# Reordering of raw weight buffers, of the next tokens' splits and of the output tokens' last scaling at a block's seam

## The reference

```python
mod = silu(c) @ ada_w + ada_b                       # shift, scale, gate
h = rms_norm(x, norm_w) * (1.0 + scale) + shift
p = h @ w_in                                        # 1024 x 5136: gq gk gv gz glr hq hf hi hz mg
# two chunk-wise gated linear states (chunks of 64), each normed, scaled and gated: o_g, o_h
g_a, g_b = split(sigmoid(mg + merge_b))
m = g_a * (o_g @ w_up_gla) + g_b * (o_h @ w_up_hgrn)
x = x + gate * (m @ w_out)
return rms_norm(x, final_norm_w)                    # y * rsqrt(mean(y*y) + eps) * final_norm_w
```

## Time and profile before

| | us |
|---|---|
| median of 3 runs | 2870.38 |
| lowest, highest | 2867.75, 2871.15 |
| the profiled execution | 2872.56 |
| its span | 2870.8 |
| TensorE busy in it | 2812.6 (98%) |
| VectorE, ScalarE, GpSimd busy | 1649.1, 1353.0, 312.5 |
| transfers | 373.11 MB, mean 130 GB/s |
| mean granted TensorE clock | 0.992 of full speed |

### The profile page before, as it was taken

One profiled execution on the slowest core, in us unless ns is written; L12 is line 12 of the kernel. 1 busy time (PEld: TensorE's weight loads), 2 busy tenths in 40 slices (PEclk: granted clock), 3 DMA queues, 4 the chain that ended last, 5 costly groups with the idle time before them and its releaser, 6 DMA issues.

```text
span 2870.8 us, 38281 instructions
## 1 busy us (share of the span) xinstructions
PE 2812.6 (98%) x14328; PEld 2302.4 (80%) x14328; DVE 1649.1 (57%) x2122; ACT 1353.0 (47%) x1763; POOL 312.5 (11%) x415
## 2 busy tenths in 40 slices
PE   7999999999999999999999999999999999999998
PEld 4878878788887888878888888788887888888886
DVE  7765475644656455564565636646366463755636
ACT  4643347434573345633456434564345643455423
POOL 1531100101001010010100110001100011000101
PEclk9999999999999999999999999999999999999999
DMA  8532362234522345223543235422354223532234
GB/s 333 206 129 96 125 214 91 79 103 136 204 89 82 105 157 181 91 79 103 180 160 96 74 107 190 148 94 74 124 177 142 95 74 125 191 133 89 74 99 150
DMA packets 100673, 373.11 MB, mean 130 GB/s; under 512 B 11440, under 2 KB 11696, under 8 KB 98928
## 3 DMA queue, kind: packets, MB, share of 16 engines
q1 hardware_dynamic: 97040, 358.62, 37.3%
q0 software_dynamic: 3168, 11.54, 1.1%
q10 hardware_dynamic: 256, 0.20, 0.0%
HBM read 345.99 MB, written 24.12 MB: 129 GB/s over the span
## 4 chain that ended last, share of the span: by engine, by line
issue 68%; PE 23%; POOL 6%; DVE 1%; DMA 1%; ACT 0%; POOLq 0%; SPq 0%; DVEq 0%; ACTq 0%
PE F L1223 8%; PE A L1212 8%; PE A L1274 3%; POOL rstd L460 2%; PE A L1296 1%; POOL rstd L457 1%; DMA ada_w<-in_ada 1%; POOL y_rs L460 1%; PE F L1212 1%; POOL m_raw L527 0%; POOL x_rs L460 0%; POOL m_raw L529 0%; POOL m_raw L525 0%; POOL m_raw L531 0%; DVE w_lo L822 0%
## 5 line engine op out<-in xcount | busy, mean ns | idle before, releaser
L822 DVE TENSOR_TENSOR w_lo<-w_raw,w_hi 128x1024 fp32r<-128x1024 f32 x528 | 653.4, 1240 | 930.4 <-ACT w_hi L576 927.2
L576 ACT ACTIVATE w_hi<-w_raw 128x1024 fp32r<-128x1024 f32 x528 | 556.3, 1057 | 669.2 <-PE A L1212 350.1
L1223 PE MATMUL F<-h_hi,w_hi 128*128 128x512 f32 x1408 | 553.8, 393 | 0.0
L1223 PE MATMUL F<-h_lo,w_hi 128*128 128x512 f32 x1408 | 548.2, 389 | 0.0
L1223 PE MATMUL F<-h_hi,w_lo 128*128 128x512 f32 x1408 | 548.2, 389 | 0.0
L1212 PE MATMUL A<-w_hi,h_hi 128*128 128x512 f32 (+1 forms) x1408 | 533.3, 379 | 0.0
L1212 PE MATMUL A<-w_lo,h_hi 128*128 128x512 f32 (+1 forms) x1408 | 523.7, 372 | 0.0
L1212 PE MATMUL A<-w_hi,h_lo 128*128 128x512 f32 (+1 forms) x1408 | 522.9, 371 | 0.0
L1212 PEld LDWEIGHTS A<-w_hi,h_hi 128*128 128x128 f32 x1408 | 264.9, 188 | 55.8 <-issue 8.7
L1223 PEld LDWEIGHTS F<-h_hi,w_hi 128*128 128x128 f32 x1408 | 264.4, 188 | 56.1 <-ACT gates L690 1.4
L1223 PEld LDWEIGHTS F<-h_lo,w_hi 128*128 128x128 f32 x1408 | 264.4, 188 | 55.5 <-issue 1.7
(11 more groups left out here) (215 smaller groups left out, 3533.7 us busy)
## 6 DMA issues: line engine op xcount, KB each, us to landing
w_raw<-in_w_stream SPq DMA_DIRECT2D x400, 512.0 KB, 3.5
w_raw<-pieces SPq DMA_DIRECT2D x112, 512.0 KB, 3.6
xy<-in_x SPq DMA_DIRECT2D x32, 512.0 KB, 6.0
result<-xy SPq DMA_DIRECT2D x32, 512.0 KB, 5.5
xf<-in_xt SPq DMA_DIRECT2D x30, 512.0 KB, 4.5
xn<-in_x SPq DMA_DIRECT2D x28, 512.0 KB, 4.4
ada_w<-in_ada SPq DMA_DIRECT2D x12, 1024.0 KB, 17.5
w_raw<-in_w_stream SPq DMA_DIRECT2D x16, 544.0 KB, 5.5
```

Source lines behind the costliest of these rows:

```text
L576: AF(w_hi[:, s % RING, 0:n], w_raw[:, r, 0:n], ACT.Copy).then_inc(w_hi_done.sem, 1)
L822: V.tensor_tensor(w_lo[:, s % RING, 0:n], w_raw[:, RAW_AT[s], 0:n], w_hi[:, s % RING, 0:n].bitcast(fp32), ALU.subtract).then_inc(w_split.s ...
L1223: last = mm(dst[:, :], w_[iw][:, s % RING, k * P:(k + 1) * P], h_[ia][:, k, :], start=(k == 0 and n == 0), stop=(k == KT - 1 and n == 2))
```

## The change

The raw buffers' order, in which the last six slots used three of the four buffers in turn, has the run of three in slots 20 to 25 instead. The next tokens' loads and sums of squares come two slots earlier. The high part of pair 1 is made in slot 61 instead of 60, by a list of its own (H_HIGH_AT), its low part in slot 62 instead of 61, and SyncE waits for it, to load pair 3, in step 65 instead of 64. The last scaling of the output tokens moves from slot 65 to slots 1 and 2 of the next block (two tiles in each); in the last block it stays at the end. The stores stay in step 3.

```diff
@@ -64,14 +64,15 @@
 STEP_AT = [GZ0 + i for i in range(8)]
 OG_AT = [24, 24, 25, 26, 28, 28, 29, 29]
 OT_AT = [28, 28, 28, 28, 29, 29, 30, 30]
-XSQ_AT = [42, 42, 45, 46]
+XSQ_AT = [40, 40, 43, 44]
 XR_AT = 48
 X_SCALE_AT = [49, 60, 65, 65]
-H_LOW_AT = [50, 61, 65, 65]
+H_HIGH_AT = [49, 61, 65, 65]
+H_LOW_AT = [50, 62, 65, 65]
 assert SLOTS == 66 and SLOTS % RING == 0
 
 
-RAW_AT = [s % RAW if s < 60 else (s - 60) % 3 for s in range(SLOTS)]
+RAW_AT = [s % RAW if s < 20 else (s - 20) % 3 if s < 26 else (s - 26) % RAW for s in range(SLOTS)]
 RAW_NTH = [RAW_AT[:s].count(RAW_AT[s]) for s in range(SLOTS)]
 RAW_NEXT = [next(n for n in range(s + 1, 2 * SLOTS) if RAW_AT[n % SLOTS] == RAW_AT[s]) for s in range(SLOTS)]
 
@@ -387,18 +388,19 @@
                         if RAW_NEXT[s] == OUT0:
                             sp.wait_ge(pieces_out, PIECES * 16)
                         load_w(RAW_NEXT[s] % SLOTS)
-                    if s in (39, 40) and not last:
-                        load_x(b + 1, s - 39)
-                    if s == 45 and not last:
+                    if s in (37, 38) and not last:
+                        load_x(b + 1, s - 37)
+                    if s == 43 and not last:
                         for t in (2, 3):
                             sp.wait_ge(x_sq.sem, x_sq.at(b + 1, t - 1))
                             load_x(b + 1, t)
                     if s in (50, 51) and not last:
                         sp.wait_ge(x_sq.sem, x_sq.at(b + 1, s - 47))
                         load_pair(b + 1, s - 50)
-                    if s in (54, 64) and not last:
-                        sp.wait_ge(h_split.sem, h_split.at(b + 1, s // 10 - 4))
-                        load_pair(b + 1, s // 10 - 3)
+                    if s in (54, 65) and not last:
+                        n = 1 if s == 54 else 2
+                        sp.wait_ge(h_split.sem, h_split.at(b + 1, n))
+                        load_pair(b + 1, n + 1)
                     if s in (54, 56):
 
                         if s == 54:
@@ -792,7 +794,7 @@
                                     act.wait_ge(ssq_done.sem, ssq_done.at(b, 8))
                                 x_square(b + 1, t)
                         for j in range(4):
-                            if s == X_SCALE_AT[j]:
+                            if s == H_HIGH_AT[j]:
                                 h_high(b + 1, j)
                     if s == SLOTS - 1:
                         for t in (2, 3):
@@ -937,6 +939,13 @@
                 cols_ = slice(n * 512, (n + 1) * 512)
                 V.tensor_tensor(gate_bc[:, cols_], F[n][:, :], gate_bc[:, cols_], ALU.add).then_inc(mg_used.sem, 8)
 
+            def final_scale(b, n):
+
+                t = n % NT
+                dve.wait_ge(y_rstd.sem, y_rstd.at(b, n + 1))
+                V.scalar_tensor_tensor(out=xy(t), in0=xy(t), scalar=y_rs[:, t:t + 1], in1=fnw_bc[:, :],
+                                       op0=ALU.mult, op1=ALU.mult).then_inc(y_ready.sem, 1)
+
             def over_tiles(row, n):
 
                 return row.unsqueeze(1).broadcast_to([P, NT, n])
@@ -1135,12 +1144,12 @@
                         for j in range(4):
                             if s == H_LOW_AT[j]:
                                 h_low(b + 1, j)
-                    if s == SLOTS - 1:
-                        for t in range(NT):
-                            dve.wait_ge(y_rstd.sem, y_rstd.at(b, t + 1))
-                            V.scalar_tensor_tensor(out=xy(t), in0=xy(t), scalar=y_rs[:, t:t + 1],
-                                                   in1=fnw_bc[:, :], op0=ALU.mult,
-                                                   op1=ALU.mult).then_inc(y_ready.sem, 1)
+                    if s in (1, 2) and not first:
+                        for t in (0, 1) if s == 1 else (2, 3):
+                            final_scale(b, t - NT)
+                if last:
+                    for t in range(NT):
+                        final_scale(b, t)
                 assert last or link_at[1] == DVE_LINKS, f"DVE_LINKS {link_at[1]}"
 
             body(0, False, first=True)
```

## The result

The changed kernel takes 2848.91 us (median of 4, 2845.69 to 2851.12) against 2870.77 for the kernel before: ratio 0.9926, 95% interval 0.991 to 0.9942, so 17 to 26 us saved where 12 were forecast; the time lies 2 us under the range. The profiled execution took 2851.12 us with a span of 2849.3.

A forecast was written before the change was run, and what follows sets the result against it. TensorE, busy 98% of the span, was taken as the bound, with losses at the seven seams between blocks. Savings of 5.6 + 0.65 + 1.8 + 1.0 + 2.25 = 11.3 us, plus 1.7 of clock, gave 2858 us, range 2851 to 2865.

The forecast's parts named there:

- The additions of slot 61: Ahead of slot 64 at seven seams (block ends): split and additions come about 2.2 us earlier, TensorE's wait goes, 5.6 us.
- The buffers at the first seam: Slot 2's weights land in time, so the gap ahead of slot 3 falls from 3.08 to 2.4 us, gaining 0.65.
- the five branch gaps stay, and I leave them their 8.5: Ahead of slot 0 at seams two to six: TensorE's gaps, 2.6 us on average, and their 8.5 us clock loss remain.
- The clock: TensorE's half speed after gaps cost 11.9 us at the seams; only 1.7 us comes back, at the first seam.
- Rival 3: Clock dealt anew in the change's favour, most branch gaps losing none: 2850 us, chance 0.07.
- The sixth seam: Slot 3's split comes 1.9 us earlier against 1.69 of lateness, so its gap goes by a narrow margin: 1.8 us.
- The seventh seam: No engine branches there; without the scalings slot 3's split could be 3 us earlier, its gap gone: 2.25 us.
- The early tokens: Token loads and sums of squares two slots earlier change nothing; bounds 0 and +0.3 us per block.
- the place of the scaling: In slots 1 and 2 of the next block, two scalings (2.6 us) fit behind the split TensorE needs; cost nothing.
- the stores: Waiting in SyncE's queue for the later last scaling, they still leave slot 8's weights at least 2 us; cost nothing.
- the buffers in slots 20 to 25: The run of three buffers there covers 16 us, while a load lands in 3.5 us; cost nothing.
- Rivals 1, 2 and 4: Additions stay late, 2863.5, chance 0.10; slot 3 stays late, 2865, 0.07; stores delay weight loads in SyncE's queue, 2884, 0.03.

The follow-up runs named there:

- high_only: Kernel before with only pair 1's high part in slot 61, low part in slot 62 and pair 3's load one step later: 2858.02 us, ratio 0.9949.
- late_pass: Changed kernel with one more TensorE wait, at the head of slot 65, for the split of slot 0's weights: 2864.64 us, 0.9979 of the kernel before.
- scale_only: Kernel before with only the last scaling moved to slots 1 and 2 of the next block: 2864.59 us, ratio 0.997.
- no_early: Changed kernel with the next tokens' loads and sums of squares back at their old slots: 2849.06 us, 0.9917 of the kernel before.
- squares_later: Changed kernel with ScalarE's last two sums of squares behind its copy for slot 3, block 0 written out on ScalarE: 2841.44 us, 0.9891 of the kernel before.
- three_line: Changed kernel with the blocks of TensorE, ScalarE and VectorE written out instead of looped: 2832.33 us, 0.9871 of the kernel before.

## Why the prediction was wrong

The direction was right, the size was not: 12 us forecast, 21.9 measured. In terms of the profiled executions the forecast was 2859.6 and the measurement 2851.12.

- **The additions of slot 61: right.** The wait is gone at all seven seams, by the mechanism described (VectorE idle 0.18 us instead of 2.35).
- **The buffers at the first seam: right.** The gap became 2.41 us (forecast 2.4), with the clock at 0.88 behind it (forecast: gives back 1.7 us).
- **"The change has no part in that branch", and "the five branch gaps stay, and I leave them their 8.5": this is the step that failed.** I took the gap as a fixed price of the branch, because five gaps agreed on it within 0.3 us. It is what sticks out of a branch that starts while 13 matmuls (17 in the changed kernel) are still to run, once TensorE's sequencer is past its last wait. The same edit that freed slot 61's additions moved slot 65's split from F−3.3 to F−5.6, and the branch's start from F−3.0 to F−3.96. high_only shows it from one side, late_pass from the other. Idle at the branch is 6.6 + 2.1 instead of 12.9 us; with 0.16 us more for each of eight gaps instead of five, 3.7 us less.
- **The clock**, hanging on the same step: I left 10.2 us, 3.4 are lost. That is 6.8 us, most of the miss. Rival 3 had this outcome with a chance of 0.07, but as luck with unchanged gaps. It is not the luck of one profile: the mean granted clock over the four executions of the changed kernel is 0.996, over 21 of the kernel before on the first chip 0.9936, and the difference is worth 6.8 us too. The gaps got shorter and split: those of 1.74 us and less here lost nothing, those of 2.07 us (fifth seam) and 2.41 us (first) read 0.88. How much of the 6.8 us the shorter gaps explain is not settled, since scale_only lost only 6.8 us in all with gaps of 2.6 to 2.8 us.
- **The sixth seam: wrong the other way.** "Gone by a narrow margin" assumed that TensorE arrives 2.9 us late; it came 0.4 late, and 1.65 us of waiting for slot 3's weights remained. At the third seam it is 0.40. Together 2.4 us more than forecast. The other half of that sum erred less: slot 3 started at F+21.2 before, so 1.9 us earlier is F+19.3, and F+18.65 was measured. That time caps what a shorter branch gap can bring.
- **The seventh seam: right**, no gap left. **The early tokens, the place of the scaling, the stores and the buffers in slots 20 to 25: right**, no new wait of TensorE except the small ones inside slot 0, and no_early shows the first by itself. Rivals 1, 2 and 4 did not occur.

The three differences, −3.7 − 6.8 + 2.4 = −8.1, are nearly the whole 8.5 between 2859.6 and 2851.12.

## What to carry to other kernels

A gap at an engine's loop branch is not a constant: ask when the engine's sequencer passes its last wait ahead of the branch, and bring that semaphore forward. Here that helped only until the branch started at F−3.96; beyond that something else held it. At a seam add nothing up before you know which lateness covers which; removing one engine's branch or wait may only uncover the next, and may even cost, if two short idle times become one long one with the clock behind it. Writing the blocks out on TensorE, ScalarE and VectorE brought 16 us on top of the change, where the best reordering that kept the branches (squares_later) brought 8 to 10; without the change, writing out TensorE and ScalarE made the kernel slower.

## What the runs showed of the hardware

- TensorE's taken branch lasted 4.0 to 6.7 us and the one not taken 0.08 us. The gap that it left ranged from 0.24 us to 4.2 us for the same loop, by when the branch started and how long it lasted.
- Neither the branch's length nor the packet's place was the same at all seams of the changed kernel, though slot 65's split ended at F−5.6 and the branch started at F−3.9 to F−4.0 at each: the gaps are 1.59, 0.91, 1.74, 2.07 and 0.24 us. From the branch's start to slot 0's first matmul the transfer engines were busy 0.83 to 0.93 of the time, 0.86 to 0.89 in the kernel before, and 0.77 to 0.82 in late_pass, whose branches are the longest; no run varied that alone, so why the lengths differ stays open.
- The small gaps inside slot 0 go with the next packet of that queue: it begins 2.6, 1.7 and 1.5 us after slot 0's first matmul at the three seams that have one (1.19, 0.29 and 0.64 us), and 0.5 to 0.6 us after it at the two that have none.
- A wait can be charged to the wrong releaser: in late_pass the gaps at the branch are named after `xy` and `w_lo`, in the kernel before and the changed one "issue".
- Straight code of eight blocks on three engines (three_line) ran without a gap of issue on any of the three at a seam.
